# Two transformer blocks on one core: layer 0 projects the un-normed memory and x, the forget gate comes after the memory groups, and one weight part of layer 1 moves between normed chunks

## The reference

```
xn = rms_norm(h, norm_mix[i])            # h * rsqrt(mean(h*h) + eps) * g
mn = rms_norm(mem, norm_mem[i])
mk, mv = split(mn @ w_mem_kv[i])         # 4 memory heads of 64
q, k, v, f_logit, qm = split(xn @ w_in_fox[j])
log_f = log_sigmoid(f_logit + b_fgate)   # F = cumsum(log_f)
self_out = fox_attention(q, k, v, log_f) # q.k/8 + F[t] - F[s], causal, 12 heads
mem_out = memory_attention(qm, mk, mv)
h = h + concat(self_out, mem_out) @ w_out[i]
h = h + (silu(gate) * up) @ w_down[i]    # of rms_norm(h, norm_ffn[i])
```

## Time and profile before

| | |
|---|---|
| median of 3 runs | 1476.35 us (1475.97 to 1478.08) |
| the profiled execution | 1475.81 us, its span 1474.1 us |
| PE busy | 1384.3 us, 94% |
| VectorE, ScalarE, GpSimd busy | 1140.0, 771.2, 498.5 us |
| mean granted clock of PE | 0.993 |
| DMA | 542.72 MB, mean 368 GB/s |

### The profile page before, as it was taken

One profiled execution on the slowest core, in us unless ns is written; L12 is line 12 of the kernel. 1 busy time (PEld: TensorE's weight loads), 2 busy tenths in 40 slices (PEclk: granted clock), 3 DMA queues, 4 the chain that ended last, 5 costly groups with the idle time before them and its releaser, 6 DMA issues.

```text
span 1474.1 us, 25820 instructions
## 1 busy us (share of the span) xinstructions
PE 1384.3 (94%) x8468; PEld 1071.8 (73%) x8468; DVE 1140.0 (77%) x2751; ACT 771.2 (52%) x1800; POOL 498.5 (34%) x600
## 2 busy tenths in 40 slices
PE   9999999999999999999999989988999988888888
PEld 8888999999889999998898986444454433333333
DVE  6666888787777888778789769788777778787764
ACT  6656544446556444457786544444444454444443
POOL 1111011110111111010111025667667666767672
PEclk9999999999999999999999998999999999999999
DMA  9999899999999999999999958999999999999997
GB/s 354 346 342 343 287 394 394 398 390 355 343 351 363 336 396 400 396 394 350 325 341 330 356 183 318 386 400 403 406 405 403 396 407 408 401 403 409 407 399 307
DMA packets 141598, 542.72 MB, mean 368 GB/s; under 512 B 22655, under 2 KB 22799, under 8 KB 128064
## 3 DMA queue, kind: packets, MB, share of 16 engines
q0 software_dynamic: 101904, 396.41, 71.9%
q1 hardware_dynamic: 39168, 142.97, 25.8%
q10 hardware_dynamic: 432, 2.19, 0.4%
HBM read 576.08 MB, written 135.27 MB: 483 GB/s over the span
## 4 chain that ended last, share of the span: by engine, by line
PE 55%; DMA 20%; DVE 11%; issue 5%; POOL 4%; ACT 4%; POOLq 0%; DVEq 0%; ACTq 0%
PE PS L747 10%; PE PS L743 10%; PE PS L738 9%; DMA late<-expert_uv,idx 9%; DMA attn<-expert_uv,idx 4%; DMA attn<-expert_u,idx 4%; PE PS L1242 3%; PE PS L871 3%; PE PS L980 3%; PE PS L769 3%; PE PS L984 3%; PE PS L985 3%; DVE late L2481 2%; DMA ada<-w_ada 2%; DVE attn L2481 2%
## 5 line engine op out<-in xcount | busy, mean ns | idle before, releaser
L1344 ACT ACTIVATE early_splits<-ring 128x1024 fp32r<-128x1024 f32 x166 | 175.4, 1057 | 121.9 <-PE PS L738 96.5
L1769 DVE TENSOR_TENSOR early_splits<-ring,early_splits 128x1024 fp32r<-128x1024 f32 x166 | 202.6, 1221 | 33.0 <-ACT early_splits L1344 32.8
L2481 DVE CUSTOM_DVE_ANT_0 late<-late,PS 128x1024 f32<-128x1024 f32 x125 | 151.8, 1215 | 61.4 <-DMA late<-expert_uv,idx 61.0
L1686 ACT ACTIVATE gel<-dot 128x1 f32<-128x1 f32 x256 | 51.8, 202 | 280.3 <-DVE dot L2481 279.7
L2481 DVE CUSTOM_DVE_ANT_0 attn<-attn,PS 128x1024 f32<-128x1024 f32 x125 | 151.9, 1215 | 35.5 <-DMA attn<-expert_uv,idx 28.3
L1242 PE MATMUL PS<-late,wrg 128*128 128x512 f32 x284 | 135.9, 605 | 19.4 <-ACT wrg L1679 19.1
L1242 PE MATMUL PS<-attn,wrg 128*128 128x512 f32 x288 | 133.7, 595 | 6.3 <-ACT wrg L1679 5.1
L1279 PE MATMUL PS<-late,wrg 128*128 128x512 f32 x208 | 102.1, 614 | 32.3 <-ACT wrg L1679 32.2
L670 POOL DMA_INDIRECT attn<-expert_u,idx x93 | 88.1, 947 | 101.5 <-DVE idx L2433 73.1
L680 POOL DMA_INDIRECT attn<-expert_v,idx_v x93 | 92.8, 998 | 73.8 <-issue 25.2
L1242 PEld LDWEIGHTS PS<-late,wrg 128*128 128x128 f32 x284 | 51.6, 192 | 89.1 <-issue 89.0
(11 more groups left out here) (444 smaller groups left out, 3381.7 us busy)
## 6 DMA issues: line engine op xcount, KB each, us to landing
ring<-wstream SPq DMA_DIRECT2D x258, 512.0 KB, 9.1
expert_uv<-expert_u POOLq DMA_DIRECT2D x64, 1024.0 KB, 14.1
expert_uv<-expert_v POOLq DMA_DIRECT2D x64, 1024.0 KB, 15.9
ada<-w_ada POOLq DMA_DIRECT2D x32, 512.0 KB, 10.1
late<-w_ada POOLq DMA_DIRECT2D x16, 512.0 KB, 13.9
late<-wstream SPq DMA_DIRECT2D x4, 512.0 KB, 10.6
attn<-expert_u,idx POOLq DMA_INDIRECT x93, 8.7
attn<-expert_v,idx_v POOLq DMA_INDIRECT x93, 7.8
```

Source lines behind the costliest of these rows:

```text
L1344: act.activation(hi_of(u), raw(u), ACT.Copy).then_inc(hi_ready, 1)
L1769: ve.tensor_tensor(lo_of(u), raw(u), hi_of(u).bitcast(F32), ALU.subtract).then_inc(units_begun, 1)
L2481: ve.tensor_tensor_reduce(row, row, H2N[n // 8], 1.0, 0.0, ALU.mult, ALU.add, dot[:, n % 2, k:k + 1]).then_inc(dot_ready, 1)
```

## The change

In layer 0 the projections start from MEM and X times their gain vectors only; the factor per token (RM or RS) is applied to the results. Keys and queries are taken from PSUM by VectorE with this factor (`take_scaled`), values by ScalarE with a factor per partition (`take_values`), for which two tiny matmuls with a stationary part of RM or RS put the factor on the partitions (`scale_by_token`). VectorE makes the squares of MEM, ScalarE those of X later, summed by VectorE in three additions and by PE in one matmul inside qm0. km0, the gate and the qm tiles do their fine activations before their fine weights. Unit 0 is issued from ScalarE's queue ahead of X. The forget gate's ScalarE part goes from step 0 to 5, its VectorE parts to 3 and 6, FQ's transposes to step 6 (bank 6), its copy to step 7. PE no longer waits for the constants ahead of step 0. In layer 1, fine part `at + 3` goes between chunks 3 and 4 of the norm; there the rest is as it was.

```diff
-        for u in range(at, at + PROJ_UNITS[layer]):
-            if u == 0:
+        for u in range(max(at, 1), at + PROJ_UNITS[layer]):
+            if u == 1:
                 sp.wait_ge(mem_landed, 16)
...
+    def split_T(out, u, i, xh, xl, hi_waits=None, lo_waits=None, fine_first=False, between=None):
+        def fine_activations(last):
+            for k in range(KC):
+                if lo_waits is not None:
+                    pe.wait_ge(lo_waits, due(lo_waits))
+                mm = pe.matmul(out, hi_of(u)[:, k * P:(k + 1) * P], xl[:, k, :], start=False,
+                               stop=last and k == KC - 1)
+            return mm
...
+        if fine_first:
+            fine_activations(False)
+        if between is not None:
+            between()
         pe.wait_ge(units_begun, u + 1 if i is None else i * RING + (u + 1))
         for k in range(KC):
...
+            mm = pe.matmul(out, lo_of(u)[:, k * P:(k + 1) * P], xh[:, k, :], start=False,
+                           stop=fine_first and k == KC - 1)
+        return mm if fine_first else fine_activations(True)
...
+    def scale_by_token(q, rs):
+        pe.wait_ge(scale_ready, q + 1)
+        begin(6)
+        for b in range(NB):
+            mm = pe.matmul(PS[:, 6, 2 * b:2 * b + 2], rs[:, b * P:(b + 1) * P], first_row[:], start=True, stop=True)
+        mm.then_inc(tile_for["act"], handed(6, "act"))
...
+    def chunk_sum(bank, src=SQ, units=ones[:, 0:P], steps=KC - 1):
...
+        pe.wait_ge(summed, due(summed, steps))
         begin(bank)
...
+        pe.matmul(PS[:, bank, 0:T], units, src[:, 0, :], start=True, stop=True).then_inc(
...
+        scaled_by = "act" if layer else "vec"
+        proj(bank["km", 0], at, mem, (mh_ready, ml_ready), by=scaled_by, fine_first=layer == 0)
...
             norm_sum(NORM_BANK, SQ, KC)
-        proj(bank["km", 1], at + 1, mem)
-        taken["km", 1] = made["act"]
+        proj(bank["km", 1], at + 1, mem, by=scaled_by)
         pair_half(bank["vm", 1], at + 2, 0, mem)
+        if layer == 0:
+            scale_by_token(0, RM)
         pair_half(bank["vm", 1], at + 3, 1, mem)
...
         if layer == 0:
-            proj(bank["gate", 0], at + 4, x, fresh)
+            proj(bank["gate", 0], at + 4, x, fresh, by=scaled_by, fine_first=True)
...
         before, earlier = None, None
-        if layer == 0:
-            pe.wait_ge(const_loaded, 16)
...
-                proj(bank[kind, c], u, x, fresh)
+                proj(bank[kind, c], u, x, fresh, by=scaled_by, fine_first=layer == 0 and kind == "qm",
+                     between=(lambda: chunk_sum(7, SQ, start_units, 3)) if (layer, s) == (0, 0) else None)
...
+            taken[kind, c] = made["act" if kind == "v" else scaled_by]
+            if kind == "qm":
+                pair_taken[layer, 6 + c] = ((scaled_by, taken[kind, c]), ("act", taken["vm", 1]))
...
+                if (kind, c) == (("v", p + 1) if p % 2 == 0 else ("k", p)):
+                    pair_taken[layer, p] = ((scaled_by, taken["k", p]), ("act", taken["v", p | 1]))
+            if layer == 0 and (kind, c) == ("qm", 1):
+                scale_by_token(1, RS)
+            if layer == 0 and (kind, c) == ("q", 1):
                 pe.wait_ge(fcum_ready, due(fcum_ready))
-                begin(FQ_BANK)
+            attend(layer, group_at[s], before, earlier)
+            if layer == 0 and (kind, c) == ("q", 1):
                 for b in range(NB):
                     mm = pe.transpose(PS[:, FQ_BANK, b * P:(b + 1) * P], FT[:, b * P:(b + 1) * P], ident)
                 mm.then_inc(tile_for["vec"], handed(FQ_BANK, "vec"))
-            attend(layer, group_at[s], before, earlier)
             before, earlier = group_at[s], before
...
     start_busy(STARTING)
     pe.wait_ge(units_set, 1)
-    norm_sum(0, SQ, KC, units=start_units)
+    pe.wait_ge(row_set, 1)
+    norm_sum(3, SQ, KC, units=start_units)
     start_busy(2)
-    norm_sum(3, XN, KC, units=start_units)
-    start_busy(4)
...
     act.dma_start(MEM[:], mem_t).then_inc(mem_landed, 16)
     act.dma_start(col[:], cols).then_inc(cols_loaded, 16)
+    act.dma_start(ring[:, 0:D], wstream[0][:, 0:D]).then_inc(unit_landed[0], 16)
     act.dma_start(X[:], x_t).then_inc(x_loaded, 16)
     act.wait_ge(blank_set, 1)
...
     def forget_gate():
-        act.wait_ge(took["act"], own(took["act"]))
+        act.wait_ge(fgate_ready, 1)
...
         act.activation(spl[:, 1, :], spl[:, 1, :], ACT.Ln, bias=1.0).then_inc(sp_ln, 1)
+        early_table(ACT.Exp, 1)
...
+        def take_values(cols, src, q):
+            act.wait_ge(tile_for["act"], due(tile_for["act"]))
+            for b in range(NB):
+                ins = act.activation(V[:, b, cols], src[:, b, :], ACT.Copy, scale=token_scale[:, q, b:b + 1])
+            ins.then_inc(took["act"], one(took["act"]))
+        def take_scale(q):
+            take(token_scale[:, q, :], PS[:, 6, 0:2 * NB].rearrange("p (b j) -> p b j", b=NB)[:, :, 0])
+            act.wait_ge(took["act"], own(took["act"]))
+        if layer == 0:
+            split_hi(at + 5)
+            take_scale(0)
+            take_values(slice(768, D), value_tile("vm", 1), 0)
+            split_hi(at + 6)
+            std(7, D)
+            early_table(ACT.Exp, 2)
+        else:
+            split_hi(at + 2)
+            take(KT[:, 6, :], tile("km", 0))
             early_table(ACT.Sqrt)
             std(3, D)
-        split_hi(at + 3)
-        if layer == 0:
+            split_hi(at + 3)
+            take(KT[:, 7, :], tile("km", 1))
+            split_hi(at + 4)
             chunks_hi(XH, XN, normed, xh_ready)
-        take(KT[:, 7, :], tile("km", 1))
-        split_hi(at + 4)
-        if layer:
-            chunks_hi(XH, XN, normed, xh_ready)
-        take(V[:, :, 768:D], value_tile("vm", 1))
-        split_hi(at + 5)
-        if layer == 0:
-            split_hi(at + 6)
-            take(FY[:], tile("gate", 0), ACT.Identity, bias=colv("b_f"))
+            take(V[:, :, 768:D], value_tile("vm", 1))
+            split_hi(at + 5)
...
             split_hi(FUSED_AT[layer] + s + 2)
-            if layer == 0 and s == 0:
+            if layer == 0 and s == 5:
                 forget_gate()
-            if kind == "q":
+            if layer == 0:
+                if (kind, c) == ("qm", 1):
+                    take_scale(1)
+                elif kind == "v" and c % 2:
+                    take_values(slice((c // 2) * T, (c // 2 + 1) * T), value_tile("v", c), 1)
+            elif kind == "q":
                 take(QT[:, c, :], tile("q", c), scale=DH ** -0.5)
...
     act.wait_ge(mem_landed, 16)
-    squares(MEM)
-    std(0, D, RM)
+    act.wait_ge(cols_loaded, 16)
+    for c in range(KC):
+        act.activation(MEMH[:, c, :], MEM[:, c, :], ACT.Copy, scale=colv("norm_mem0", c)).then_inc(mh_ready, 1)
+    split_hi(0)
+    std(3, D, RM)
+    split_hi(1)
+    split_hi(2)
+    split_hi(3)
     act.wait_ge(x_loaded, 16)
-    squares(X, dst=XN)
-    split_hi(0)
-    std(3, D)
-    chunks_hi(MEMH, MN, mem_normed, mh_ready)
-    split_hi(1)
-    act.wait_ge(cols_loaded, 16)
+    for c in range(KC):
+        act.activation(XH[:, c, :], X[:, c, :], ACT.Copy, scale=colv("norm_mix0", c)).then_inc(xh_ready, 1)
+    split_hi(4)
+    for c in range(KC):
+        act.activation(XN[:, c, :], X[:, c, :], ACT.Square).then_inc(residual_squared, 1)
     for layer in range(2):
...
+    def add_squares(src):
+        ve.wait_ge(residual_squared, due(residual_squared, KC))
+        for n in (4, 2, 1):
+            ve.tensor_tensor(SQ[:, 0:n, :], src[:, 0:n, :], src[:, n:2 * n, :], ALU.add).then_inc(summed, one(summed))
+            ve.wait_ge(summed, own(summed))
+            src = SQ
+    def gained_parts(dst, src, name, hi, ready, done):
+        for c in range(KC):
+            ve.wait_ge(ready, due(ready))
+            ve.scalar_tensor_tensor(dst[:, c, :], src[:, c, :], colv(name, c), hi[:, c, :].bitcast(F32),
+                                    ALU.mult, ALU.subtract).then_inc(done, one(done))
+        def take_scaled(dst, tile, rs, scale=None):
+            ve.wait_ge(tile_for["vec"], due(tile_for["vec"]))
+            src = PS[:, bank[tile], 0:T]
+            if scale is None:
+                ins = ve.tensor_tensor(dst, src, rs[:], ALU.mult)
+            else:
+                ins = ve.scalar_tensor_tensor(dst, src, scale, rs[:], ALU.mult, ALU.mult)
+            ins.then_inc(took["vec"], one(took["vec"]))
         if layer:
             split_lo(at + 2)
             invert_rms()
-            scale_norm(XN, X, gain("norm_mix1"), RS, normed)
+            scale_norm(XN, X, gain("norm_mix1"), RS, normed, range(0, 4))
             split_lo(at + 3)
-        chunks_lo(XL, XN, XH, xh_ready, xl_ready)
-        split_lo(at + 4)
-        split_lo(at + 5)
-        if layer == 0:
+            scale_norm(XN, X, gain("norm_mix1"), RS, normed, range(4, KC))
+            chunks_lo(XL, XN, XH, xh_ready, xl_ready)
+            split_lo(at + 4)
+            split_lo(at + 5)
+        else:
```

(36 more changed lines are left out.)

62 lines of the change are left out of this document (22 added, 40 removed).

## The result

| | before | after |
|---|---|---|
| first measurement, median | 1477.93 us (6 runs) | 1470.36 us (6 runs, 1469.10 to 1471.61) |
| its ratio | | 0.9948, 95% interval 0.9934 to 0.9961 |
| measured again, median | 1478.68 us (17 runs) | 1474.30 us (11 runs, 1471.85 to 1478.48) |
| its ratio | | 0.9974, 95% interval 0.9964 to 0.9984 |
| profiled execution, span | 1474.1 us | 1467.5 us |

The change makes the kernel faster, by 7.6 us in one measurement and 4.4 in the other; 7.0 was forecast. The two intervals don't quite meet (0.9961 and 0.9964), and this difference is the second question of this text. The start comes first.

A forecast was written before the change was run, and what follows sets the result against it. PE had 55% of the last-ending chain, DMA 20%; the change touches the first 65 us, where PE lacks work, and one spot of layer 1. 6.9 + 0.85 - 0.7 + 0 = 7.0; 1476.35 - 7.0 = 1469.3 us, 80% within 1467.2 to 1473.4.

The forecast's parts named there:

- The start: Layer 0's first projections: first projection at 10.7 instead of 15.50, q0 near 33.5 instead of 40.40, 6.9 us earlier.
- rival B: Start late by the weight stream: unit 2 lands at 17.4, costing 2.6 to 4.8 us (1471.9 to 1474.1); chance 0.10.
- the first two terms of the sum: Layer 0's first block: 6.9 us from the earlier q0 plus 0.85 from its vanished wait for a fine part.
- The forecast of the upper clock level: New start: PE stays at the upper clock level throughout; one more fall would lose 1.7 us.
- The gate: Forget gate at its new steps: logs and FT hidden, but v1's values taken late on ScalarE, 0.7 us lost.
- Rival A: Gate's ScalarE queue decides: half to all of 5.2 us open at step 6, less 0.7; 1471.5 to 1473.8; chance 0.13.
- Its variant: Gate on ScalarE: each of two table loads costs twice its 1.28, 2.6 us more, 1471.9; chance 0.04.
- The takes on VectorE: 14 query and key tiles moved to VectorE, about 0.48 us each, lie in its idle time and cost nothing.
- Rival C: VectorE's takes lie on the score chain: 12 steps x 0.68 = 8.2 us, so slower at 1477.5; chance 0.04.
- Layer 1: Moved fine part: wait of 1.02 goes, 0.9 comes at qm0's second pass; gain 0.1 (-0.3 to +1.0), taken as 0.
- So its copies leave 20.9 of the first slack and the rest as it was.: GpSimd's queue: of 27.85 us idle before its first w_ada copy of the loop, 20.9 stays; the end doesn't move.
- rival D: First loop, full of transfers, absorbs the gain as w_ada or joined rows arrive when they did: 1476.3; chance 0.07.

The follow-up runs named there:

- b_l1_alone: The kernel before with only the layer-1 reorder (fine part at+3 between normed chunks 3 and 4); 1478.80 us, one run.
- gate_split: Changed kernel with the forget gate's absolute value and exponents on ScalarE in step 4, logarithms still in step 5; 1477.08 us, one run.
- start_late: Changed kernel with 26 more filler matmul pairs ahead of the first projection; median 1476.30 us, ratio 0.9985.
- gate_back: Changed kernel with the forget gate's ScalarE part back in step 0 and VectorE's parts in steps 0 and 1; median 1476.46 us, ratio 0.9974.
- after_again: The changed kernel, unaltered, measured again; median 1474.30 us, ratio 0.9974.
- l1_undone: Changed kernel with layer 1's norm chunks and fine part in their old order; 1474.26 us, ratio 0.996.
- take_twice: Changed kernel with a second, unused copy of each of the 14 query and key tiles on VectorE; median 1473.13 us, ratio 0.9955.
- unit0_sp: Changed kernel with unit 0 issued from SP's queue after MEM has landed, as before; 1469.58 us, one run.
- no_x_gate: Changed kernel without SP's wait for X ahead of issuing unit 2; 1470.06 us, one run.
- l1_fine_first: Changed kernel with layer 1's first memory-query tile doing its fine activations before its fine weights; 1470.04 us, one run.
- best: Changed kernel without unit 2's wait for X, with layer 1's qm0 fine activations first and the forget gate split over steps 4 and 5; 1471.16 us, ratio 0.9944.

## Why the prediction was right, and where it was not

**The start** went as listed: km0 10.51 (10.7), fine pass 13.04 (13.2), unit 2 seen by ScalarE at 14.98 (14.3), first scores 33.19 (33.5), RS ready at 31.57 (31.3). X landed at 11.35, not 10.7; unit 2, issued then, took the 3.6 of the sum. PE had slack for most of this 0.7 and waited 0.31 at 17.45, so rival B does not decide. (Its upper price of 4.8 left out the 0.5 of slack that it names; 4.3 is what its terms give.) The cause that B names, X before unit 2, is there, and moves the first scores by up to 1.0 between executions. q0 came 6.6 earlier (6.9), and its wait of 0.85 went: k0 came 7.5 earlier. v1 came 7.70 earlier (47.25, not 54.95), near the first two terms of the sum, 7.75, but 0.2 of that is the FQ transposes, which have left the step ahead of it. The forecast of the upper clock level throughout the new start came true. What the dip had cost in the old one, "up to 1.7", did not reach q0: b_l1_alone, without the dip, reached q0 no sooner.

**The gate** cost 1.0 of that up to k1 (63.26 to 56.56 is 6.70 earlier): 0.51 is the wait, and it was forecast as 0.7, at this instruction and with this releaser. gate_split shows that 0.8 in all hung on the place in ScalarE's queue (v1 to k1 takes 8.51 there, 9.31 in after, 8.31 before), since the instructions behind the late scores were late too; the other 0.2 is the FQ transposes, now in this step, and only gives back what their leaving had won. Rival A would have cost 2.2 to 4.5. Its variant, in which each table load costs twice its row, is refuted: the next activations start 0.02 and 0.01 after the loads of 1.28 end (51.88 to 51.90 and 53.71 to 53.72), and in gate_split again. The drain of about 1.38 us of the Trainium skill (ScalarE: Activation LUTs, What ACT_TABLE_LOAD costs) shows in no row here, neither ahead of a load nor behind it.

**The takes on VectorE** cost nothing, not even twice. Rival C is refuted.

**Layer 1** gave 0.1 to 0.2 of the block, no more than the block varies (124.4 or 124.5 with the same code), taken as 0: the wait only moved, to the place that the count of VectorE's list had given (353.5 + 0.96, waiting 0.9; it waits 0.93).

**The end is where a step failed**: "So its copies leave 20.9 of the first slack and the rest as it was." The slack was 12.07, in other executions with the new start down to 5.39. The sum moved the time at which VectorE asks for w_ada by the gain, but left the time at which GpSimd's 26 paced joins are through. These wait for copies, not for VectorE ("<-DMA" in the row at 154.68). The last of them left at 154.68 and not at 145.58, while the loop needs w_ada 6.7 sooner. Why it left later is in part open. The joins begin later (24.86, not 22.37), but that isn't it: in start_late they begin at 25.05 and the last leaves at 148.99. That they share full DMA engines with a weight stream that is used faster would fit start_late, but not gate_back, whose output projection is nearly as late (115.2) and whose last join leaves at 156.76. The windows of 150 to 190, before and then after, show what that used up:

```profile
150.00:170.00 20.00, 20.00 (x168) 19.95 (x167) 15.29 (x20) 11.65 (x18) 0.00 (x0) 1.00 0.88 305
170.00:190.00 20.00, 20.00 (x170) 20.00 (x169) 16.69 (x26) 8.99 (x12) 2.74 (x5) 1.00 0.87 293
```

```profile
150.00:170.00 20.00, 20.00 (x170) 20.00 (x169) 15.17 (x24) 10.15 (x14) 2.85 (x6) 1.00 1.00 385
170.00:190.00 20.00, 20.00 (x170) 20.00 (x169) 16.33 (x28) 9.19 (x13) 2.73 (x5) 1.00 1.02 370
```

Before, the DMA engines had 12% and 13% of 40 us free there, 5 us; after, nothing.

A join takes 14.0 or 15.6 us to land (medians of its two kinds in after). With under some 15 us of slack, by these durations, the last ones are still under way when the loop's first w_ada copies are issued, and these take longer: the median landing of the ada<-w_ada copies from 150 to 200 is 8.8 us before, 9.4 in start_late and 9.2 in gate_back, 10.4 in after, 11.7 in after_again, 13.7 in l1_undone and 15.7 in gate_split. The table, in the order of the slack, has the first loop at 204.4 to 205.5 for the seven executions with a slack of 12 and more, at 205.8 to 206.5 for the four with 8.15 to 10.89, and at 208.7 to 209.8 for the three below 8. So the first loop's length goes with the slack, which is better evidence than the output projection alone gives.

The four kernels whose output projection comes after 115 have loops of 204.7 to 205.5 and 191.1 to 191.6 (means 205.1 and 191.3); the other ten have 204.4 to 209.8 and 191.0 to 193.4 (means 206.6 and 192.2). That is 1.5 + 0.9 = 2.4 lost on average, by single executions of different kernels: an estimate of a third of the gain, in some executions none of it and in others over half (gate_split's loop is 5.1 longer than before's, the clock's part in it). So rival D was not an alternative to the forecast but, by this estimate, a part of the truth, and that the first measurement came out at 7.6, so near the forecast, is in part luck. start_late, with the same code but a later start, has the slack and a short loop back, which speaks for this cause. Shown are the slower copies, the waits behind them and the full engines; that the joins still under way are what slows them was not tried by itself, with fewer than 26 joins ahead of the loop, say.

**The difference between the two measurements** is explained by this only in small part, as far as one profiled execution of each can tell. These executions, after and after_again, are 4.6 apart (1467.5 and 1472.1). The output projection is 0.4 earlier in after_again, the first loop 2.1 longer, the second 0.8 shorter, the stage ahead of the expert rows 0.5 longer, and the expert stage 3.3 longer (603.0, not 599.7). This last stage, which the change doesn't touch, takes 599.2 to 603.1 over the fourteen executions, on average 602.0 in the four with a late output projection and 601.4 in the other ten. It doesn't go with the start, then, and its 1.7 under the kernel before are chance in the 6.6 that the first pair of profiles shows. Why it varies stays open; its shortest two (take_twice, after) are also those with the least time at the clock's lower level in it, 7.1 and 9.6 us, the others have 10.1 to 19.6.

The stage ahead of it moves too, but not with the start either. From the second loop's end to the first expert row before took 218.2 and after 219.7. By the granted clock unit0_sp has no stretch at the lower level there and takes 217.1; with one of 3.4 us (before, l1_undone, no_x_gate, l1_fine_first) it is 218.2 or 218.3, with 6.8 in all 219.7 to 220.2 in five kernels and 221.2 in best, with 10.2 (start_late, take_twice, gate_split) 221.2.

## What to carry to other kernels

Count a start by the lists of all engines, and put what the start outruns (here the forget gate) behind work that hides it; this gave every milestone of the first block within 0.7 us. Where the DMA engines are full, a gain of compute time can be paid out of the slack of the copies: compare not only who waits for whom in a queue, but when its transfers can be through at the bandwidth that is left. And read a small edit by the length of its own stretch in the trace, beside several executions of the unaltered code, as its total can hide under a stage that varies by more: here the 0.4 of no_x_gate was no more than the start's own variation.

## What was not expected of the hardware

Identical code varies in place. The first feed-forward loop took 204.4 us in one execution of the changed kernel and 206.5 in another, its expert stage 599.7 and 603.0, and the two measured ratios of this kernel to the one before differ by 0.26%. Part of it is the clock: in the stage between the second loop and the expert rows, where the same instructions run in every kernel, the lower level came for 0, 3.4, 6.8 or 10.2 us, and the stage took 217.1 with none and 221.2 with 10.2, which is 1.4 for each 3.4. In the first 200 us it came behind holes of PE of about 3 us (gate_back at 40, gate_split at 189), while the new start's holes of 0.35 and 0.31, and one of 1.45 in unit0_sp, brought none. The old start's hole of 0.75 near 18 had it behind it in the kernel before and not in b_l1_alone, where the same instructions run.
